# Four column blocks in place of three in the last stage of a hybrid conv/RWKV-7 step

## What is computed

```python
    bonus = (jnp.sum(rh * (hd(kd[:, :, 0]) + hd(kd[:, :, 1])) * r_k, -1, keepdims=True)) * vh
    ys = y_fwd + y_bwd
    mu_y = jnp.mean(ys, -1, keepdims=True)
    var_y = jnp.mean(jnp.square(ys - mu_y), -1, keepdims=True)
    yg = ((ys - mu_y) * lax.rsqrt(var_y + GN_EPS)).reshape(bn, t, W_C)
    yg = yg * p['gn_g'].astype(jnp.float32) + p['gn_b'].astype(jnp.float32)
    yc = (yg + bonus.reshape(bn, t, W_C)).astype(dt) * jax.nn.silu(gc)
    out = jnp.concatenate([ya, yb, yc], -1) @ p['w_out']
    x = x + gate * rms_norm(out, p['g_post'])
```

## Time and profile before

| | |
|---|---|
| median of 3 runs | 1164.47 us (1164.07 to 1166.47) |
| the profiled execution | 1167.99 us, of which the span is 1166.3 us |
| PE busy over the span | 90% |
| last stage | from 1007 us to the end of the span |

### The profile page before, as it was taken

The page is one execution under the profiler, slowest core; times in us unless marked ns, Lnnn a source line. Parts: engine busy times, 40 slices in busy tenths (PEclk is TensorE's granted clock), DMA queues, the critical chain, the costliest instruction groups (busy, mean ns, idle before and its releaser), DMA issues. The chain is left out here.

```text
span 1166.3 us, 31957 instructions
## 1 busy us (share of the span) xinstructions
PE 1051.2 (90%) x14387; PEld 923.5 (79%) x14387; DVE 649.6 (56%) x919; ACT 420.1 (36%) x688; POOL 419.6 (36%) x384
## 2 busy tenths in 40 slices
PE   4869999899978999998479999999999998789997
PEld 0359888799977988996469998999999997456685
DVE  0480001966847331134368887888888885365532
ACT  3241110110114234312246554655655563443321
POOL 6071111021110432221156555555666664142110
PEclk9879999999989999999579999999999999879999
DMA  9601233211111311000000000000000000461231
GB/s 375 205 0 37 72 113 113 72 37 37 37 37 26 109 56 37 1 1 1 10 2 4 4 4 12 4 4 4 4 4 4 4 4 3 164 235 37 72 108 55
DMA packets 29956, 61.46 MB, mean 53 GB/s; under 512 B 3296, under 2 KB 21364, under 8 KB 28666
## 3 DMA queue, kind: packets, MB, share of 16 engines
q1 hardware_dynamic: 28332, 54.17, 13.4%
q10 hardware_dynamic: 1488, 5.24, 1.2%
HBM read 49.68 MB, written 9.73 MB: 51 GB/s over the span
## 5 line engine op out<-in xcount | busy, mean ns | idle before, releaser
L610 PE MATMUL ps<-input_rounded,weights_rounded 128*128 128x386 f32 x768 | 265.3, 345 | 10.0 <-DVE zc L780 4.7
L612 PE MATMUL ps<-input_rounded,weights_rest 128*128 128x386 f32 x768 | 261.4, 340 | 0.0
L611 PE MATMUL ps<-input_rest,weights_rounded 128*128 128x386 f32 x768 | 261.4, 340 | 0.0
L1295 POOL TENSOR_TENSOR arena<-arena,lvl 128x512 f32<-128x512 f32 x108 | 139.8, 1309 | 76.7 <-ACT arena L1212 47.0
L610 PEld LDWEIGHTS ps<-input_rounded,weights_rounded 128*128 128x128 f32 x768 | 146.2, 190 | 18.0 <-issue 12.6
L413 POOL TENSOR_TENSOR weights_rest<-arena,weights_rounded 128x2048 fp32r<-128x2048 f32 x16 | 75.9, 4744 | 207.8 <-ACT weights_rounded L459 207.8
L611 PEld LDWEIGHTS ps<-input_rest,weights_rounded 128*128 128x128 f32 x768 | 146.2, 190 | 0.7 <-issue 0.3
L612 PEld LDWEIGHTS ps<-input_rounded,weights_rest 128*128 128x128 f32 x768 | 146.3, 190 | 0.0
L1011 PE MATMUL ps<-arena 64*64 64x64 f32 x2880 | 107.0, 225 | 18.3 <-issue 14.6
L1011 PEld LDWEIGHTS ps<-arena 64*64 64x64 f32 x2880 | 95.5, 138 | 24.0 <-issue 17.1
L1021 PE MATMUL ps<-arena 64*64 64x64 f32 x2880 | 106.7, 226 | 5.3 <-DVE arena L1421 4.8
(11 more groups left out here) (223 smaller groups left out, 1761.5 us busy)
## 6 DMA issues: line engine op xcount, KB each, us to landing
arena<-in_w_in SPq DMA_DIRECT2D x16, 1024.0 KB, 5.2
arena<-in_ada_w SPq DMA_DIRECT2D x12, 1024.0 KB, 6.8
mix_scratch<-zc SPq DMA_DIRECT2D x4, 1158.0 KB, 8.7
out<-arena SPq DMA_DIRECT2D x9, 512.0 KB, 2.6
zc<-in_x_sample ACTq DMA_DIRECT2D x2, 2048.0 KB, 19.5
zc<-in_w_out SPq DMA_DIRECT2D x4, 1024.0 KB, 8.2
arena<-in_x_sample SPq DMA_DIRECT2D x8, 512.0 KB, 3.5
zc<-mix_scratch SPq DMA_DIRECT2D x1, 2316.0 KB, 18.9
```

What stands on the lines that cost most here:

```text
L610: pe.matmul(o, w_hi[:, k, cut], hi_of_h[:, k, cols_b], start=(k == 0), stop=False)
L611: pe.matmul(o, w_hi[:, k, cut], lo_of_h[k][:, cols_b], start=False, stop=False)
L612: last = pe.matmul(o, w_lo[:, k, cut], hi_of_h[:, k, cols_b], start=False, stop=(k == KT - 1))
L1295: pool.tensor_tensor(Um[l % 3], UT, lvl[:, l, :].unsqueeze(1).to_broadcast([P, 2 * PAIRS, C]), ALU.mult).then_inc(q_um[l], 1)
```

## The change

The borders become 0, 132, 388, 772, 1158: the first block is split into one of 132 columns (padding and the prompt's tokens, output 0) and one of 256 (outputs 1 and 2). The other two blocks keep their columns and are now the third and the fourth. Since there are four blocks, everything that is done per block is done four times, and the order of the calls is written anew on PE, ACT and DVE. In this text the blocks after the change are called b0 (132), b1 (256), b2 (384) and b3 (386).

```diff
-        BLOCK_ENDS = (0, TS + 2 * P, TS + 5 * P, W)
+        BLOCK_ENDS = (0, TS, TS + 2 * P, TS + 5 * P, W)
...
-        needs = [4 * (i // 3 + 1) for i in range(9)]
+        needs = [4 * (b + 1) for b in (0, 1, 1, 2, 2, 2, 3, 3, 3)]
+        NK = len(CUTS)
...
                 statistics(0)
                 spreads(0)
+                statistics(1)
                 output(0)
-                statistics(1)
+                spreads(1)
                 output(1)
-                spreads(1)
+                statistics(2)
                 output(2)
-                statistics(2)
+                spreads(2)
                 output(3)
-                spreads(2)
-                for i in range(4, 9):
+                statistics(3)
+                output(4)
+                spreads(3)
+                for i in range(5, 9):
                     output(i)
...
+                begin(0)
+                deviation(0)
+                round_w_out(0)
+                scale(0)
+                begin(1)
+                round_inputs(0)
+                round_w_out(1)
+                round_w_out(2)
+                round_w_out(3)
+                deviation(1)
+                end(1)
+                mean_square(0)
...
+                begin(0)
+                invert(0)
+                for n in range(4):
+                    normalise(n)
+                begin(1)
+                for n in range(4):
+                    gate(n)
+                for n in range(4):
+                    rest(n)
+                for c in range(1, WO_PARTS):
+                    rest_of_w_out(dve, c)
+                invert(1)
+                end(1)
+                dve.wait_ge(s_gg, 16)
+                finish(0)
+                begin(2)
+                finish(1)
+                invert(2)
+                end(2)
```

More of the change, by code:

```diff
@@ L1518, in hybrid_step_kernel @@
         first_col = [TP if i == 0 else TS + P * (i - 1) for i in range(9)]
-        needs = [4 * (i // 3 + 1) for i in range(9)]
-        s_gl = [sem(f"gate_c_landed_{b}") for b in range(NB)]
+        needs = [4 * (b + 1) for b in (0, 1, 1, 2, 2, 2, 3, 3, 3)]
+        NK = len(CUTS)
+        s_gl = [sem(f"gate_c_landed_{b}") for b in range(NK)]
         s_wo = [sem(f"w_out_landed_{c}") for c in range(WO_PARTS)]
@@ L1585, in _ @@
                 sp.dma_start(yab, mix_dram[0:4].rearrange("m p w -> p m w")).then_inc(s_ab, 16)
-                load_gate(1)
-                load_gate(2)
+                for b in range(1, NK):
+                    load_gate(b)
                 sp.dma_start(gg, gate_dram[:, :].unsqueeze(0).to_broadcast([P, 2, D_MODEL])).then_inc(s_gg, 16)
@@ L1726, in round_inputs, with begin, scale, end @@
                     act.activation(yab_hi[:, :, cut], yab[:, :, cut], ACT.Copy).then_inc(f_ah, 1)
[L1728 to L1737, removed]
+                def begin(b):
+                    bonus_keys(4 * b)
+                    for n in range(4 * b, 4 * b + 4):
+                        square(n)
+                        if n < 4 * b + 3:
+                            bonus_keys(n + 1)
+                def scale(b):
                     for n in range(4 * b, 4 * b + 4):
                         affine(n)
+                def end(b):
+                    scale(b)
                     round_inputs(b)
[L1741 to L1750, removed]
+                begin(0)
[11 more added lines that the diff above has]
+                begin(2)
+                mean_square(1)
+                deviation(2)
+                end(2)
+                mean_square(2)
+                begin(3)
+                mean_square(3)
+                deviation(3)
+                end(3)
+                for i in range(4, 9):
                     mean_square(i)
@@ L1811, in rest, with begin, end @@
                     dve.tensor_tensor(y_lo[:, a, cut], y[:, a, cut], y_hi[:, a, cut].bitcast(F32), ALU.subtract).then_inc(f_yl, 1)
[L1813 to L1817, removed]
-                        centre(n)
[L1819 to L1824, removed]
+                def begin(b):
+                    for n in range(4 * b, 4 * b + 4):
+                        centre(n)
+                def end(b):
+                    for n in range(4 * b, 4 * b + 4):
                         normalise(n)
@@ L1829, in _ @@
                     gate(4 * b + 3)
-                    for n in group:
+                    for n in range(4 * b, 4 * b + 4):
                         rest(n)
[L1832 to L1835, removed]
+                begin(0)
[13 more added lines that the diff above has]
+                finish(0)
+                begin(2)
+                finish(1)
+                invert(2)
+                end(2)
+                finish(2)
+                begin(3)
+                finish(3)
+                invert(3)
+                end(3)
+                for i in range(4, 9):
                     finish(i)
```

## The result

The changed kernel takes 1180.88 us (median of 4 runs, 1179.5 to 1183.39) against 1165.07 us before (median of 4 runs); the ratio of the runs is 1.0126, 95% interval 1.0103 to 1.015. By the medians it is slower by 15.8 us, by the ratio by 14.7. The forecast was 1181.6, in a range of 1175.5 to 1187.

What follows compares the result with a forecast made beforehand. It took output 0's end plus 113.93 us of unbroken PE work to set the end. Start -1.4, uncovered waits +14.1 and clock +4.4 summed to +17.1 us, from a median of 1164.47 to 1181.6 us, range 1175.5 to 1187.

Steps and rivals of the forecast that it cites:

- The waits behind the spreads: PE ahead of outputs 1 and 3: b1's and b2's chains uncovered, 7.0 + 9.7 + 2.62 in place of 2 x 2.62, +14.1 us.
- The clock: Outputs 1 and 3: each wait lowers PE's clock, about 12 slow matmuls, 2.2 us each; +4.4 us, bounds 0 and 6.8.
- The start: Last stage up to output 0's end: smaller first block lets branches land earlier; -1.4 us, bounds -2.5 and +0.5.
- DVE's run lasts until 1040.2: Weight rests for output 0: DVE starts after ACT's rounding at 1030.1 and takes 10.02 us, as before.
- its quarters start one after the other: Sign of being right, in output 0: its quarters start as DVE's 3.4 us steps end.
- A sign of being wrong: Output 0 ending well before 1042 would mean the weight rests started without waiting for the branches.
- What held output 0 before: Kernel before: output 0's end, 1045.00, held by weight rests, whose last came 0.86 us before the last quarter.
- Nothing else on the path: Added block's 12 instructions each on PE, ACT and DVE and one load add nothing; tail as before.
- The clock stays up: Rival at both waits: exposed, but one or both restarts unpaid; 1177.2 us with neither paid, 1179.4 with one; chance 0.16.
- only b2's wait: Rival: b1's spreads done inside output 0's waits, so only b2's chain is exposed; +7.9, 1172.4 us; chance 0.04.
- not slower: Rival: early start outweighs waits, needing output 0 to end by 1026.5, 18.5 us earlier; chance 0.03, of which 0.02 faster.
- the longer start: Rival: b1's statistics at low clock ahead of output 0 delay it to 1045.5 or later; 1185.5 us; chance 0.09.

Runs made afterwards that it cites:

- filled waits: Changed kernel with 19 idle-filling matmuls between b1's spreads and output 1, and 27 between b2's spreads and output 3: 1176.28 us.
- the third experiment: Changed kernel with b2's and b3's statistics moved ahead of outputs 1 and 3, and b1's spreads ahead of output 0: 1166.32 us.
- the last one: Changed kernel with statistics of b2 directly behind b1's spreads, and ACT and DVE alternating steps of b1's chain and b2's statistics: 1165.75 us.
- POOL's cut in two: Three-block kernel before, with POOL's branch rest split: 132 columns first, 256 after DVE's three weight rests: one run, 1166.81 us.
- POOL kept busy: Changed kernel with an added POOL subtraction of 1024 columns ahead of the branches' rest for b0: 1183.52 us.

## Why the prediction was right

The mechanism and its two places were as forecast. One term of the sum was mis-sized, the start, and the clock's, too small by less, balanced part of it.

- **The waits behind the spreads, forecast +14.1.** Measured 7.11 + 9.71 + 2.62 in place of 2 x 2.62: +14.2. b1's chain was put at 7.0 and took 7.11, so scaling each step by its columns with its fixed part kept was good to 0.1 us for the whole chain. Covering them, alone and together, gave back 11.5, 6.3 and 14.6 us. This is shown.
- **The clock, forecast +4.4.** Against the same kernel with filled waits: +5.0. The first 12 matmuls took 5.29 us behind b1's chain, and 13 took 5.71 behind b2's. The first matmul after a wait is itself longer (0.59 us to the next one). The Trainium skill, page "TensorE: Matmul & The Clock Gate", section "What's actually happening", has 6, 11 and 14 slow matmuls, counted at a kernel's start; the 12 and 13 here lie inside.
- **The start, forecast -1.4 with bounds -2.5 and +0.5. The step that failed.** Output 0 ended 33.93 us after the stage's start in place of 37.95: -4.0, outside the bounds. "DVE's run lasts until 1040.2" took the 10.02 us of three weight rests as a property of the rests. It was one of 5.6 us, held up by POOL's subtraction of 1552 columns, and two of 2.3. In the new order POOL subtracts 528 columns and is through (1026.66 + 1.34) before DVE's run starts at 1028.42, and the run takes 6.70 us. The start of the run was right: forecast at 1030.1, 23.05 us after the stage's start, and measured 23.10 after it, behind the branches' rounding. So the only wait inside output 0 is the 1.60 us for the first rest, and from 1030.77 on its 36 matmuls run through. The sign that its quarters start one after the other as DVE's steps of 3.4 us end did not come. Adding POOL's work back gave the run its 10 us again and took 3.1 us of the 4.0, of which some 0.8 was an effect of its own.
- **A sign of being wrong.** Output 0 ended at 1039.25, or 1041.0 if the stage is put where it started before, and so ahead of the 1042 named as a sign that the rests had not waited for the branches. They had: ACT rounded the branches as soon as they landed (1025.94), and DVE's run began behind the rounding of weight part 1. The early end came from the shorter run.
- **What held output 0 before.** The prediction says that the rests held its end. In the kernel before PE ran from 1031.46 to 1045.00 without a pause, and the last rest was there 0.86 us before its quarter began. What held the end was the start, 1031.46, the low clock, and PE's own 48 matmuls; the rests hold it only in the new order.
- **Nothing else on the path.** -4.0 + 14.2 + 5.0 is 15.2, against 15.1 measured. The fourth block's own work is free as far as the runs can tell: with both chains covered the ratio is 1.0006 (0.9995 to 1.0017). The output behind b3's spreads still takes the 0.3 us more than others that the one behind the second block's spreads took before.
- **The rivals.** "The clock stays up" is out; so is "only b2's wait", and "not slower" for want of 18.5 us. b1's statistics did run partly at the low clock, the condition of the longer start, but ACT was through with what stands ahead only 0.34 us before the branches landed, so this was hidden by a narrow margin.

The number came closer than its working. The sum was +17.1 and the stage grew by 15.1. But the medians lie 15.8 us apart, and the kernel before had a median of 1165.07 beside the changed one, 0.6 above the one that the forecast counted from. That 1181.6 is only 0.7 us from 1180.88 is in part luck.

Where did the 4.0 us of the earlier output 0 go in the kernels with everything covered? In the third experiment PE does b1's spreads ahead of output 0 and waits 2.75 us for their reciprocal, and output 0 ends at 37.6 us. In the last one it ends at 33.7 us, but the spreads of b1 and the short waits stand behind it, and output 1 starts only 0.4 us earlier than before.

## What to carry to other kernels

On an engine that runs in order, a step that feeds a chain through other engines has to be followed by work that doesn't need the chain. Before cutting blocks finer, count for each such step which consumers of the previous block are left to stand behind it; here a block with a single output left none. Price an uncovered chain by its length from first issue to last result, and add the restart at the lower clock. When a group's mean comes from a few instructions, read each of them before scaling it: 3.3 us a piece was 2.3, 5.6 and 2.3.

## What the runs showed of the hardware

- A DVE subtraction of 2048 columns with both inputs in SBUF takes 2.28 us alone. POOL's subtractions take 3.51 us for 1536 columns, 2.42 for 1024 and 1.34 for 528 where DVE's rests don't run beside them. Beside each other they took turns. The one that started first took its own time, and the other ended about its own time after that. The last column but one is the time from the end of the neighbour that had started before to the instruction's own end:

| kernel | instruction | start to end | took | neighbour ended | from there | alone |
|---|---|---|---|---|---|---|
| before | POOL, 1552 | 1031.54 to 1036.99 | 5.45 | 1033.60 | 3.39 | 3.5 (1536) |
| before | DVE, second rest | 1033.52 to 1039.14 | 5.62 | 1036.99 | 2.15 | 2.28 |
| POOL's cut in two | POOL, 528 | 1030.49 to 1033.74 | 3.25 | 1032.56 | 1.18 | 1.34 |
| POOL's cut in two | DVE, second rest | 1032.48 to 1035.90 | 3.42 | 1033.74 | 2.16 | 2.28 |
| POOL kept busy | POOL, 1024 | 1029.01 to 1033.43 | 4.42 | 1031.19 | 2.24 | 2.42 |
| POOL kept busy | DVE, second rest | 1031.11 to 1035.58 | 4.47 | 1033.43 | 2.15 | 2.28 |
| POOL kept busy | POOL, 528 | 1033.39 to 1036.74 | 3.35 | 1035.58 | 1.16 | 1.34 |
| POOL kept busy | DVE, third rest | 1035.50 to 1038.89 | 3.39 | 1036.74 | 2.15 | 2.28 |

The Trainium skill, page "SBUF — State Buffer", section "Who interferes with whom", says that a DVE instruction with two SBUF inputs contends with a GpSimd instruction that reads SBUF; the runs agree.

- The clock was half for most of b0's statistics though PE shows no idle time in them: from 1007.24 to 1011.51 the mean is 0.60 at 4.27 of 4.27 us busy. The first block's statistics of the earlier trace rows ran at 1.00 throughout. It was half again at the start of b1's, behind the wait of 2.37 us and the short spreads, and rose within them. Ahead of both first statistics PE had been idle for the same 2 us (1.99) behind the barrier. All seven kernels with four blocks show this fall within the first statistics, and neither of the two with three blocks does. No run isolates what makes the difference, and the cause stays open:

```profile
1005.32:1007.24 1.92, 1.77 (x9) 1.17 (x9) 0.88 (x3) 1.20 (x4) 1.16 (x2) 1.00 0.47 58
1007.24:1011.51 4.27, 4.27 (x17) 2.50 (x16) 1.47 (x5) 1.77 (x6) 0.00 (x0) 0.60 0.98 399
...
1016.62:1020.40 3.78, 3.78 (x8) 1.97 (x8) 1.27 (x3) 1.95 (x6) 3.78 (x5) 0.50 1.05 385
1020.40:1025.10 4.70, 4.70 (x17) 1.86 (x16) 2.79 (x9) 2.13 (x8) 0.42 (x1) 0.94 1.03 399
```

- In the changed kernel waits of 1.03 and 1.60 us ahead of and within output 0 left the clock at 1.00; those of 4.81 and 6.62 us didn't. With POOL kept busy the same two waits were 1.04 and 1.81 us, and the second quarter of output 0 then ran at a mean of 0.63:

```profile
1031.24:1035.85 4.61, 4.61 (x12) 3.31 (x12) 4.61 (x2) 1.59 (x2) 4.61 (x2) 0.63 1.01 409
```
